# SSD output products of two heads issued in turn, in a hybrid decoder step on one Trainium2 core

## The reference

```python
cb = jnp.einsum('bcqgn,bcsgn->bcqsg', cc, bc)
y_diag = jnp.einsum('bcqsgk,bcsgkp->bcqgkp', cb[..., None] * decay_in, xs)
...
y_off = jnp.einsum('bcqgn,bcgkpn->bcqgkp', cc, h_prev) * jnp.exp(a_cum)[..., None]
return (y_diag + y_off).reshape(bsz, l, g, k, p), h_last
```

## Time and profile before

| | |
|---|---|
| median of three executions | 2014.29 us (2006.54 to 2016.28) |
| the profiled execution | 2010.78 us, its span 2009.4 us |
| PE busy | 1922.3 us, 96% of the span |
| DVE, ACT, POOL busy | 670.7, 377.5, 498.7 us |
| mean granted clock of TensorE | 0.958 of 2.4 GHz |
| first y product of chunk 0, last y product of the samples | start at 607.4 and 805.6 us |

### The profile page before, as it was taken

How to read it: one execution, slowest core, us unless ns; L and a number is a source line. 1 busy time by engine, 2 the same in 40 slices (tenths; PEclk the granted TensorE clock), 3 DMA queues, 4 the chain that set the end, 5 groups by cost and what they waited for, 6 DMA issues and landing times.

```text
span 2009.4 us, 28522 instructions
## 1 busy us (share of the span) xinstructions
PE 1922.3 (96%) x11504; PEld 1819.6 (91%) x11504; DVE 670.7 (33%) x1402; ACT 377.5 (19%) x938; POOL 498.7 (25%) x489
## 2 busy tenths in 40 slices
PE   5989989999999999989999999999999999999996
PEld 5988889999997778867879999999999999999996
DVE  5866401132703231466566425111111211111124
ACT  4211143111112221243230213110011001101111
POOL 3751112222221111011112223223222322232231
PEclk9978889999999998879899999999999999999998
DMA  6371154322231212333325432223322332333233
GB/s 216 89 124 64 53 123 162 97 94 84 94 109 64 84 66 75 95 112 107 95 97 192 138 106 68 89 94 118 102 94 84 122 109 84 104 126 97 91 112 132
DMA packets 80606, 209.29 MB, mean 104 GB/s; under 512 B 14240, under 2 KB 33952, under 8 KB 80264
## 3 DMA queue, kind: packets, MB, share of 16 engines
q1 hardware_dynamic: 31136, 86.19, 13.7%
q0 software_dynamic: 20880, 76.03, 12.2%
q10 hardware_dynamic: 28504, 45.88, 7.4%
HBM read 182.68 MB, written 24.48 MB: 103 GB/s over the span
## 4 chain that ended last, share of the span: by engine, by line
PE 85%; DMA 4%; ACT 3%; DVE 3%; ACTq 2%; POOL 2%; issue 1%; POOLq 0%; DVEq 0%
PE ps L1027 24%; PE ps L1028 24%; PE ps L1029 24%; DMA WH<-in_w 3%; PE ps L1387 1%; POOL WL L803 1%; PE ps L1333 1%; ACT BTAB L1561 1%; PE ps L1335 1%; PE ps L1222 1%; PE ps L1225 1%; PE ps L1310 1%; DMA U<-u_scratch 1%; PE ps L1463 1%; PE ps L1464 1%
## 5 line engine op out<-in xcount | busy, mean ns | idle before, releaser
L1027 PE MATMUL ps<-HL,WH 128*128 128x384 f32 (+1 forms) x2520 | 838.6, 333 | 20.5 <-ACT GT L1528 10.5
L1028 PE MATMUL ps<-HH,WL 128*128 128x384 f32 (+1 forms) x2520 | 825.6, 328 | 0.0
L1029 PE MATMUL ps<-HH,WH 128*128 128x384 f32 (+1 forms) x2520 | 823.9, 327 | 0.0
L1027 PEld LDWEIGHTS ps<-HL,WH 128*128 128x128 f32 x2520 | 483.1, 192 | 34.3 <-issue 28.9
L1028 PEld LDWEIGHTS ps<-HH,WL 128*128 128x128 f32 x2520 | 483.5, 192 | 0.2
L1029 PEld LDWEIGHTS ps<-HH,WH 128*128 128x128 f32 x2520 | 482.8, 192 | 0.0
L803 POOL TENSOR_TENSOR WL<-WRAW,WH 128x1024 fp32r<-128x1024 f32 x141 | 340.7, 2416 | 522.9 <-DMA WH<-in_w 522.9
L800 POOL DMA_DIRECT2D WH<-in_w x141 | 81.3, 576 | 904.2 <-PE ps L1029 892.9
L1913 DVE TENSOR_TENSOR FM<-FS,ps 128x384 f32<-128x384 f32 (+1 forms) x66 | 34.3, 521 | 437.5 <-PE ps L1029 433.5
L1027 PE MATMUL ps<-FL,WH 128*128 128x384 f32 (+1 forms) x528 | 172.4, 327 | 6.6 <-POOL WL L803 6.4
L1028 PE MATMUL ps<-FH,WL 128*128 128x384 f32 (+1 forms) x528 | 170.6, 323 | 0.0
(11 more groups left out here) (309 smaller groups left out, 1748.3 us busy)
## 6 DMA issues: line engine op xcount, KB each, us to landing
WRAW<-in_w SPq DMA_DIRECT2D x145, 512.0 KB, 3.3
WH<-in_w POOLq DMA_DIRECT2D x141, 512.0 KB, 3.7
gate_scratch<-GT ACTq DMA_DIRECT2D x24, 528.0 KB, 3.0
PX<-gate_scratch ACTq DMA_DIRECT2D x24, 528.0 KB, 3.8
X<-in_x ACTq DMA_DIRECT2D x8, 528.0 KB, 4.3
X<-in_x SPq DMA_DIRECT2D x16, 192.0 KB, 6.8
u_scratch<-UF ACTq DMA_DIRECT2D x4, 528.0 KB, 2.7
GF<-gelu_scratch ACTq DMA_DIRECT2D x4, 528.0 KB, 6.5
```

What stands on the lines that cost most here:

```text
L1027: nc.tensor.matmul(out, wh, rl, start=start, stop=False)
L1028: nc.tensor.matmul(out, wl, rh, start=False, stop=False)
L1029: return nc.tensor.matmul(out, wh, rh, start=False, stop=stop)
```

## The change

The loop over eight heads becomes a loop over four pairs of heads 2i and 2i+1. In a pair the two products of `XS` with `L` come first, then the two of `HS` with `CD`; in the sample chunk the eight sequences follow, with the two heads in turn for each. The fence stands in front of pair 2, that is in front of head 4 as before. No product, operand or semaphore is added or removed.

```diff
-            for h in range(8):
-                g, k, i, r = h // 4, h % 4, h // 2, 64 * (h % 2)
-                if h == 4:
+            for i in range(4):
+                g = i // 2
+                heads = [(2 * i + j, (2 * i + j) % 4, bank[7][64 * j:64 * j + 64, i * P:i * P + rows]) for j in range(2)]
+                if i == 2:
                     fence(last)
-                o = bank[7][r:r + 64, i * P:i * P + rows]
-                m = L[0:rows, h, 0:rows] if not smp else LS[:, 1, h, :]
-                nc.tensor.matmul(o, XS[0:rows, h * HD:(h + 1) * HD], m, start=True, stop=smp)
+                for h, k, o in heads:
+                    m = L[0:rows, h, 0:rows] if not smp else LS[:, 1, h, :]
+                    nc.tensor.matmul(o, XS[0:rows, h * HD:(h + 1) * HD], m, start=True, stop=smp)
                 if not smp:
-                    last = nc.tensor.matmul(o, HS[64 * g:64 * g + 64, n % 2, k, :], CD[64 * g:64 * g + 64, k, :],
-                                            start=False, stop=True)
+                    for h, k, o in heads:
+                        last = nc.tensor.matmul(o, HS[64 * g:64 * g + 64, n % 2, k, :], CD[64 * g:64 * g + 64, k, :],
+                                                start=False, stop=True)
                 else:
                     for b in range(NSEQ):
-                        last = nc.tensor.matmul(o[:, b:SMP:NSEQ], H0[64 * g:64 * g + 64, b, k, :],
-                                                CD[64 * g:64 * g + 64, 0, k * SMP + b:(k + 1) * SMP:NSEQ],
-                                                start=False, stop=True, skip_group_check=True)
+                        for h, k, o in heads:
+                            last = nc.tensor.matmul(o[:, b:SMP:NSEQ], H0[64 * g:64 * g + 64, b, k, :],
+                                                    CD[64 * g:64 * g + 64, 0, k * SMP + b:(k + 1) * SMP:NSEQ],
+                                                    start=False, stop=True, skip_group_check=True)
```

## The result

The change made the kernel faster: 1979.56 us in the median of four executions (1977.47 to 1983.14), against 2013.47 us before; the ratio is 0.9845, with a 95% interval from 0.9819 to 0.9872, a gain of 1.3 to 1.8%. The forecast was 1983. The profiled execution took 1977.47 us, its span 1976.1 us.

A forecast was written before the change was run, and what follows sets the result against it. PE, busy for 96% of the span, was taken to bound the kernel. Prompt chunks' 22.6 us plus the samples' 8.6 gave 31.2; 2014.29 - 31.2 = 1983.1, stated as 1983 us, range 1973 to 1994 us.

The forecast's parts named there:

- Prompt chunks: y products of each prompt chunk: 3.08 us in place of 5.90, a gain of 2.82; eight chunks give 22.6 us.
- Sample chunk: y products of the samples: 5.9 us in place of 14.48 with the clock falling after 3.9 us, gain 8.6.
- Around the samples: Gate behind the sample products: its 3.05 us at half clock shrink to about 1.5 only if the clock does not fall.
- The total: Whole kernel: 22.6 + 8.6 = 31.2 us of gain, 1.5%.
- What is late next: Work around the y products: nothing becomes late, edits cost nothing; without that cover, at most 0.6 us more per chunk.
- slow rival: y products: the odd head's load waits for the even head's pass; 13 us or more slower, 2027 us; chance 0.03.
- The step that was mis-sized: y products of prompt chunks: a change between 128 and 64 rows costs 0.04 us, 2.6 in all for 64.
- first rival: y products: the change overlaps nothing, only 64 changes of rows fall away, gain 2.6 us, 2012 us; chance 0.05.
- denser case: y products: half as many row changes, loads run ahead; up to 43 us gain, 1971, likely about 1976 us; chance 0.05.
- fully dense stream: Prompt chunk's y products, bound not taken: 32 passes at 0.054 us, 1.7 us; gain 4.05 with the fence kept.

The follow-up runs named there:

- prompt chunks alone: Heads paired in the eight prompt chunks only, the sample chunk in the old order, against the kernel before: median 1989.03 us, ratio 0.9913.
- pairs of the same half: Against the kernel before: prompt chunks pair heads writing the same half, in order L, L, CD, CD; samples in old order: median 2001.74 us, ratio 0.9956.
- groups of four: Against the kernel before: L products of four heads, then their CD products; fence waited for behind the second group's L products: 1968.2 us, ratio 0.9805.

## Why the prediction was right

Step by step, in the order of the prediction:

- *Prompt chunks*: 3.08 us and a gain of 2.82 were forecast; 3.08 and 2.82 were measured in all eight. The price of two products side by side, one step plus 0.01, came from L1347, and that reading held for both kinds of product.
- *Sample chunk*: 5.9 us with a fall of the clock after 3.9 us was forecast; it took 5.77, and the clock fell after 4.4. The gain was 8.7 in place of 8.6.
- *Around the samples* the sum kept the stage in front and the 3.05 us of the gate at half clock as before. The gate stood at half the clock for 5.49 us, and its 24 matmuls took 6.88 us in place of 5.78; the stage in front was 1.5 us longer. This was within the range and not foreseen, but nothing shows that the change caused it: with the samples in the old order these two stages took 18.03 and 6.87 us (prompt chunks alone) or 19.57 and 6.47 (pairs of the same half).
- *The total*: the stages of the change gave 31.3 us against 31.2 forecast. The medians moved by 33.9; the difference is scatter of other stages, and it happened to help.
- *What is late next*: nothing, as argued. The 16.94 us between a state product and the next y products are the same in both kernels. The reading of PE's waits had overlooked one, 1.3 us once in front of chunk 0's y products; it is 1.3 us in both kernels, so the sum doesn't suffer.
- *The slow rival*, with loads that wait for the other half's matmuls, is out: the windows show four loads begun in the first 0.15 us, while the first pass of each half was still running. The rule of the Trainium skill that it rested on (page "TensorE: Matmul & The Clock Gate", section "Part 3: Packing small matmuls — row/col tiling") does not hold here, where the rows are the same and the columns differ.
- *The step that was mis-sized* stands in the first rival: "such a change costs 0.04 us". I took it from the start of one pass to the next, 0.20 - 0.16, and overlooked that the 0.16 of a first pass was itself a consequence of the change. The run with pairs of the same half showed 0.11 for a pass where nothing changes, so a change costs 0.14. Had nothing overlapped, the gain of the prompt chunks would have been 9 us and not 2.6 for the whole. In the forecast the error didn't show, since its step of 0.36 holds both the change and the two passes.
- *The denser case* was placed in the wrong kernel. The changed kernel keeps its changes of rows, and the groups of four, which halve them, reach 2.34 us a chunk; the prediction's fully dense stream, which no run reached, was 1.7.

That the two halves at the same time and the fewer changes of rows make the gain is shown by the runs. Why a change of rows costs what it does, and what sets the look-ahead of three passes, stays open.

## What to carry to other kernels

Where products use part of the array's columns, put those with the same rows of the array next to each other and let the halves of the output partitions take turns, every one or two products: two then cost what one did. Count the changes of rows too: here each cost 0.14 us whether or not halves overlap, and grouping by four added 6.3 us, a fifth of the change's gain, to it. Put a wait for an own earlier product behind other work that doesn't depend on it.

## What was not expected of the hardware

- The other half starts ahead only by a little: with runs of 16 passes of 4 columns, and with runs of 8, a half's first pass began when 3 of the other half's were left; with runs of 4 passes the overlap was nearly full.
- A fall of the clock cost 4.1 us in one execution of one chunk (the run of the prompt chunks alone) where the other profiled executions had none.
- The first y product began between 602.4 us (groups of four) and 611.3 us (pairs of the same half), though nothing in front of it differs between these kernels. This scatter, 9 us, is as large as the gain of some experiments, and stages compare far more sharply than whole times. PE was busy for 550.5 us of that stretch in the one and 554.3 in the other (from 27.30 us on), so less than half of the 9 us is a slower PE; where the rest comes from is open.
